# Four edits to the front of a two-block transformer kernel: x laid out by features, query splits moved, eleven convolution taps as ScalarE products, modulation halves side by side

## The reference, cut to what matters

```python
mod_x = silu(c) @ w_ada + b_ada          # and the same for c_ctx: mod_c
hx = rms_norm(x, norm1_g) * (1 + sc1) + sh1
hc = rms_norm(ctx, norm1_g) * (1 + csc1) + csh1
q, k, v, u = split(hx @ w_in)            # kc, vc from hc
attn = softmax([q_rot . k_rot + bias, q . kc]) @ [v, vc]        # 8 heads of 64
conv = silu(layer_norm(depthwise_conv31(u_a * sigmoid(u_b)) + bias))
x = x + g1 * ([attn, conv] @ w_out)
```

## Time and profile before

| | us |
|---|---|
| median of 3 runs | 731.97 (731.96 to 732.14) |
| profiled execution | 731.81 |
| span from its first to its last instruction | 730.0 |
| TensorE busy | 716.6 |
| VectorE busy | 515.8 |
| ScalarE busy | 410.5 |

### The profile page before, as it was taken

The page is one execution under the profiler, slowest core; times in us unless marked ns, Lnnn a source line. Parts: engine busy times, 40 slices in busy tenths (PEclk is TensorE's granted clock), DMA queues, the critical chain, the costliest instruction groups (busy, mean ns, idle before and its releaser), DMA issues.

```text
span 730.0 us, 9710 instructions
## 1 busy us (share of the span) xinstructions
PE 716.6 (98%) x3776; PEld 575.7 (79%) x3776; DVE 515.8 (71%) x908; ACT 410.5 (56%) x693; POOL 24.9 (3%) x44
## 2 busy tenths in 40 slices
PE   7999999999999999999999999999999999999996
PEld 6678884578888888888888777778888888888885
DVE  4678999888666767756898799765857455545544
ACT  4278657986654654546545676675555344344432
POOL 1030012001000000000010000000000000000000
PEclk9999999999999999999999999999999999999999
DMA  9994939616556686744548433443376556555511
GB/s 366 414 367 142 386 109 353 216 58 237 186 186 227 231 279 198 271 152 138 161 151 300 155 116 117 148 179 135 116 231 228 175 179 203 194 174 172 173 57 58
DMA packets 72717, 144.90 MB, mean 198 GB/s; under 512 B 4112, under 2 KB 27664, under 8 KB 71648
## 3 DMA queue, kind: packets, MB, share of 16 engines
q1 hardware_dynamic: 70864, 138.98, 54.1%
q0 software_dynamic: 1520, 5.03, 2.0%
q10 hardware_dynamic: 288, 0.27, 0.1%
HBM read 143.22 MB, written 1.05 MB: 198 GB/s over the span
## 4 chain that ended last, share of the span: by engine, by line
PE 84%; DVE 6%; DMA 4%; ACT 3%; issue 2%; SPq 1%; POOL 0%; POOLq 0%; DVEq 0%
PE bank L433 22%; PE bank L435 21%; PE bank L434 21%; PE bank L754 5%; PE bank L415 4%; PE bank L752 3%; DMA WX<-in_w_ada 2%; DVE cacc L1554 2%; DMA XC<-in_ctx 1%; PE bank L452 1%; PE bank L886 1%; PE bank L908 1%; PE bank L617 1%; DVE WL L1539 1%; PE bank L751 1%
## 5 line engine op out<-in xcount | busy, mean ns | idle before, releaser
L1539 DVE TENSOR_TENSOR WL<-W,WH 128x1024 fp32r<-128x1024 f32 (+2 forms) x222 | 249.5, 1169 | 36.8 <-ACT WH L1039 36.5
L1039 ACT ACTIVATE WH<-W 128x1024 fp32r<-128x1024 f32 (+2 forms) x222 | 211.5, 1011 | 50.2 <-DMA W<-in_w_mlp 36.0
L433 PE MATMUL bank<-WH,AHL 128*128 128x512 f32 (+1 forms) x480 | 189.1, 394 | 0.3 <-DVE AHL L1548 0.3
L435 PE MATMUL bank<-WH,AHL 128*128 128x512 f32 (+1 forms) x480 | 185.4, 386 | 0.0
L434 PE MATMUL bank<-WL,AHL 128*128 128x512 f32 (+1 forms) x480 | 185.2, 386 | 0.0
L433 PEld LDWEIGHTS bank<-WH,AHL 128*128 128x128 f32 x480 | 90.2, 188 | 21.6 <-issue 3.2
L435 PEld LDWEIGHTS bank<-WH,AHL 128*128 128x128 f32 x480 | 90.1, 188 | 18.7
L434 PEld LDWEIGHTS bank<-WL,AHL 128*128 128x128 f32 x480 | 90.3, 188 | 16.9
L433 PE MATMUL bank<-WH,HH 128*128 128x512 f32 (+1 forms) x218 | 84.9, 390 | 0.0
L435 PE MATMUL bank<-WH,HL 128*128 128x512 f32 (+1 forms) x218 | 84.5, 388 | 0.0
L434 PE MATMUL bank<-WL,HH 128*128 128x512 f32 (+1 forms) x218 | 84.4, 387 | 0.0
(11 more groups left out here) (276 smaller groups left out, 853.8 us busy)
## 6 DMA issues: line engine op xcount, KB each, us to landing
W<-in_w_mlp SPq DMA_DIRECT2D x32, 1024.0 KB, 5.5
W<-in_w_in SPq DMA_DIRECT2D x24, 1024.0 KB, 5.7
W<-in_w_gate SPq DMA_DIRECT2D x22, 512.0 KB, 3.9
W<-in_w_up SPq DMA_DIRECT2D x22, 512.0 KB, 5.0
W<-in_w_down SPq DMA_DIRECT2D x11, 1024.0 KB, 4.9
W<-in_w_ada SPq DMA_DIRECT2D x10, 1024.0 KB, 9.1
WX<-in_w_ada SPq DMA_DIRECT2D x10, 1024.0 KB, 11.1
W<-in_w_out SPq DMA_DIRECT2D x8, 1024.0 KB, 5.7
```

The source lines that it names most:

```text
L433: e.matmul(po, hs, wh[:, k, c0:c0 + cw], start=first and k == 0, stop=False)
L435: ins = e.matmul(po, ls, wh[:, k, c0:c0 + cw], start=False, stop=last and k == unit.nk - 1)
L1039: e.activation(m.WH[unit.slot][:, c], m.W32[unit.slot][:, c], ACT.Copy).then_inc(S["w_hi"], 1)
L1539: e.tensor_tensor(m.WL[unit.slot][:, c], m.W32[unit.slot][:, c], m.WH[unit.slot][:, c].bitcast(F32), ALU.subtract).then_inc(S["w_lo"], 1)
```

## The change

x is laid out by features on the host and loaded so; its squares are summed over feature blocks on VectorE and over partitions by one-column matmuls, the factor is spread over partitions by two matmuls with the identity and kept as a tile, and each block is modulated from it; the shift is applied in the split. The sixteen transposes and the two scaled copies of x go. x by rows, still wanted for the residual, is loaded before unit 22. ScalarE splits the query units between the context quarters, and VectorE likewise. Eleven taps in place of eight are products; their additions come at other places among the taps. In the attention loop the two halves of a modulation step stand together behind the probability product, in the last turn the single half stands before it, and one turn of rows uses bank 0. The renaming of one semaphore is left out here.

```diff
@@ -68,6 +68,11 @@
         self.XC = M("XC", 48, [128, 2, D])
+        self.XT = M("XT", 0, [128, 8, 256])
+        self.xsq = M("xsq", 24, [128, 8, 256])
+        self.xpair = [M(f"xpair{i}", 68 + 2 * i, [128, 2, 256]) for i in range(2)]
+        self.xfour = [M(f"xfour{i}", 73 + i, [128, 256]) for i in range(2)]
+        self.rB = M("rB", 72, [128, 256])
         self.XC2 = M("XC2", 56, [128, 2, D])
@@ -186,7 +191,7 @@
-CONV_PRODUCTS = 8
+CONV_PRODUCTS = 11
 OUT_ORDER = [(2, 0), (3, 0), (0, 0), (1, 0), (2, 1), (3, 1), (0, 1), (1, 1)]
@@ -310,12 +315,14 @@
-    for tb in range(2):
-        e.dma_start(m.X[:, tb, :], d["x"][128 * tb:128 * tb + 128, :]).then_inc(S[f"l_x{tb}"], 16)
+    for h in range(2):
+        e.dma_start(m.XT[:, 4 * h:4 * h + 4, :], d["xt"][:, 4 * h:4 * h + 4, :]).then_inc(S[f"l_x{h}"], 16)
     for n in range(14):
...
     for n in range(14, len(units)):
+        if n == 22:
+            e.dma_start(m.X[:, :, :], d["x"].rearrange("(t p) n -> p t n", p=128)).then_inc(S["l_x"], 16)
         load(n)
@@ -351,8 +358,9 @@
     e.memset(m.ones[:, :], 1.0).then_inc(S["fills"], 1)
-    power(0)
-    power(1)
+    w.wait_ge(S["setup"], 2)
+    w.wait_ge(S["mean_sq"], 2)
+    e.tensor_tensor(m.stat[:, 40:42], m.stat[:, 24:26], m.stat[:, 94:95].to_broadcast([128, 2]), ALU.pow).then_inc(S["rstd"], 2)
     power(2)
@@ -479,14 +487,11 @@
         w.wait_ge(S["l_id"], 16)
-        w.wait_ge(S["x_hat"], 2)
-        for tb in range(2):
-            e.transpose(bank[b][:, 256 + tb * 128:384 + tb * 128], m.S1[:, tb, 128 * e8:128 * e8 + 128], m.ident[:, :])
         w.wait_ge(S["rows1_dve"], e8 + 1)
...
         ins.then_inc(S["rows1_turned"], 1)
-        frees(b, ("mx_dve", e8 + 1))
+        frees(b, ("mod1_sum", e8 + 1))
@@ -515,8 +520,31 @@
+    def x_sums():
+
+        for h in range(2):
+            w.wait_ge(S["x_adds"], 2 * h + 2)
+            for tb in range(2):
+                ins = e.matmul(bank[6 + tb][:, 0:1], m.xfour[h][:, tb * 128:tb * 128 + 128], m.ones[:, 0:1], start=h == 0,
+                               stop=h == 1)
+        ins.then_inc(S["sums"], 1)
+
+    def x_spread():
+
+        b = turn_bank("x_spread", 7)
+        w.wait_ge(S["l_id"], 16)
+        w.wait_ge(S["rstd"], 2)
+        for tb in range(2):
+            ins = e.matmul(bank[b][:, tb * 128:tb * 128 + 128], m.stat[:, 40 + tb:41 + tb].to_broadcast([128, 128]),
+                           m.ident[:, :], start=True, stop=True)
+        ins.then_inc(S["sums"], 1)
+        frees(b, ("setup", 5))
+
     keep_busy(16)
+    x_sums()
     mod_first(0)
+    keep_busy(3)
+    x_spread()
     mod_turn(0)
@@ -626,8 +654,8 @@
-    def mod_second_tail(i):
-        b = turn_bank("rows2_turned")
+    def mod_second_tail(i, b=None):
+        b = turn_bank("rows2_turned", b)
         w.wait_ge(S["rows2"], i + 1)
@@ -675,15 +703,19 @@
             scores1(u + 1)
+        if u in (1, 2, 3, 4, 6):
+            mod_second_tail(min(u - 1, 4), 0 if u == 6 else None)
+        if u == 5:
+            conv_mean()
+        if u == 7:
+            mod_second(11)
+        if u:
+            pv1(u - 1)
         if u < 4:
             mod_second(2 * u)
-        if u in (1, 2, 3, 4, 6):
-            mod_second_tail(min(u - 1, 4))
-        if u == 5:
-            conv_mean()
-        if u:
-            pv1(u - 1)
-        mod_second(2 * u + 1 if u < 4 else u + 4)
+            mod_second(2 * u + 1)
+        elif u < 7:
+            mod_second(u + 4)
         if u == 7:
@@ -1057,7 +1089,7 @@
         w.wait_ge(S["mx_dve"], k + 1)
-        copy(m.AH[:, k, :], m.hT[:, k, :], "mx_act")
+        e.activation(m.AH[:, k, :], m.hT[:, k, :], ACT.Identity, bias=m.mod1[:, k, 0, 0:1]).then_inc(S["mx_act"], 1)
@@ -1073,12 +1105,15 @@
+    def half_of(t, h):
+        return t[:, 4 * h:4 * h + 4, :].rearrange("p a b -> p (a b)")
+
     e.dma_start(m.cs[:, :], d["cs"]).then_inc(S["l_cs"], 16)
...
         w.wait_ge(S[f"l_x{tb}"], 16)
-        square(tb, m.X[:, tb, :], m.S1[:, tb, :])
+        e.activation(half_of(m.xsq, tb), half_of(m.XT, tb), ACT.Square, scale=1.0 / 32).then_inc(S["sq_sum"], 1)
     for k in range(6):
@@ -1094,9 +1129,11 @@
         e.activation(m.G[:, tb, :], bank[2 + tb][:, :], ACT.Sigmoid).then_inc(S["gate_sig"], 1)
-    for i in range(1, 4):
-        modulate_c(i, 3 * (i - 1))
-    hi(2)
+    hi()
+    modulate_c(1, 0)
+    hi()
+    modulate_c(2, 3)
+    modulate_c(3, 6)
     for j in range(2):
@@ -1130,7 +1167,7 @@
         from_bank("q_mm", 2 + 2 * tb, m.Q[:, tb, :], 2 + tb, slice(0, 512), "q_out", 0.125)
-    tap_products(4, 5)
+        tap_products(*((5, 6) if tb else (4,)))
     def qk_features(i, dst):
@@ -1138,8 +1175,7 @@
         from_bank("v_mm", 2 * tb + 2, m.VC[:, tb, :], 4 + tb, slice(0, 512), "vc_out")
-        if tb == 0:
-            tap_products(6, 7)
+        tap_products(*((10,) if tb else (7, 8, 9)))
     qk_features(0, m.kcT)
@@ -1593,14 +1629,15 @@
         w.wait_ge(S["mod1"], 2 * k + 2)
-        e.tensor_scalar(m.hT[:, k, :], bank[m.turn_bank["rows1_turned", k + 1]][:, 256:512], m.A1[:, 0, k:k + 1],
-                        m.mod1[:, k, 0, 0:1], ALU.mult, ALU.add).then_inc(S["mx_dve"], 1)
+        w.wait_ge(S["setup"], 5)
+        w.wait_ge(S[f"l_x{k // 4}"], 16)
+        fused(m.hT[:, k, :], m.XT[:, k, :], m.A1[:, 0, k:k + 1], m.rB[:, :], ALU.mult, ALU.mult, "mx_dve")
...
         w.wait_ge(S["mx_act"], k + 1)
-        tt(m.AL[:, k, :], m.hT[:, k, :], m.AH[:, k, :].bitcast(F32), ALU.subtract, "kx")
+        fused(m.AL[:, k, :], m.hT[:, k, :], m.mod1[:, k, 0, 0:1], m.AH[:, k, :].bitcast(F32), ALU.add, ALU.subtract, "kx")
@@ -1622,11 +1659,20 @@
     e.tensor_copy(m.csp[:, :, 0:2], m.cs[:, :].rearrange("p (k r) -> p k r", r=2)).then_inc(S["setup"], 1)
+    for h in range(2):
+        w.wait_ge(S["sq_sum"], h + 1)
+        tt(flat(m.xpair[h][:, :, :]), two(m.xsq, 2 * h), two(m.xsq, 2 * h + 1), ALU.add, "x_adds")
+        w.wait_ge(S["x_adds"], 2 * h + 1)
+        tt(m.xfour[h][:, :], m.xpair[h][:, 0, :], m.xpair[h][:, 1, :], ALU.add, "x_adds")
+    w.wait_ge(S["sums"], 1)
     for tb in range(2):
-        mean_square(tb, (tb,))
-        hat(m.X, m.S1, tb, tb, "x_hat")
+        e.tensor_scalar(col(24 + tb), bank[6 + tb][:, 0:1], EPS, None, ALU.add).then_inc(S["mean_sq"], 1)
+    rows_out(0)
+    w.wait_ge(S["sums"], 2)
+    e.tensor_copy(m.rB[:, :], bank[7][:, 0:256]).then_inc(S["setup"], 1)
     for k in range(8):
-        rows_out(k)
+        if k:
+            rows_out(k)
         modulation(k)
@@ -1645,8 +1691,9 @@
     for i in range(1, 4):
+        if i < 3:
+            lo()
         low_quarter(i, m.hTc, m.CH, m.CL, "c", ("mc_act", 3 * i))
-    lo(2)
@@ -1714,21 +1761,23 @@
     w.wait_ge(S["kc"], 4)
     w.wait_ge(S["k_out"], 2)
     rope1(m.KR, m.Kt, "rotated")
-    taps(8)
+    taps(4)
     add_product()
+    add_product()
+    taps(4)
     add_product()
     taps(8)
     lo(2)
     add_product()
-    taps(4)
+    taps(2)
     add_product()
     w.wait_ge(S["q_out"], 2)
     w.wait_ge(S["rotated"], 1)
     rope1(m.QR, m.Q, "rotated")
-    for n in range(4):
-        taps(6 if n else 2)
+    for n in range(6):
+        taps(4 if n else 0)
         add_product()
-    taps(16)
+    taps(8)
     def soft1(n):
@@ -1825,7 +1874,7 @@
             mod_second_tail(min(u - 1, 4))
-        taps((8, 7, 7, 6, 0, 0, 0, 0)[u])
+        taps((6, 6, 6, 5, 3, 0, 0, 0)[u])
         if u:
@@ -1868,6 +1917,7 @@
         hn = slice(512 * n, 512 * n + 512)
+        w.wait_ge(S["l_x"], 16)
         w.wait_ge(S["out_mm"], OUT_AT[n, tb])
@@ -2337,6 +2387,9 @@
+    def blocks(v):
+        return v.T.reshape(8, 128, 256).transpose(1, 0, 2)
+
@@ -2366,7 +2419,7 @@
-        "vec": vec, "cs": cs, "x": a["x"][0], "ctx": a["ctx"][0], "ident": np.eye(128, dtype=np.float32),
+        "vec": vec, "cs": cs, "x": a["x"][0], "ctx": a["ctx"][0], "xt": blocks(a["x"][0]), "ident": np.eye(128, dtype=np.float32),
...
```

More of the change, by code:

```diff
@@ L146 @@
 sq_sum mean_sq rstd ada1_mm rows1_dve rows1_turned mod1_sum mod1
-x_hat mx_dve mx_act kx c_hat c_turned mc_dve mc_act kc
+x_adds l_x mx_dve mx_act kx c_hat c_turned mc_dve mc_act kc
 a_mm b_mm gate_sig u u_turned hp conv_first conv k_mm q_mm v_mm k_out kc_out q_out v_out vc_out rope_mul rotated qk_turned qk_act
@@ L150 @@
 bias_zero scores1 max1 exp1 rl1 p1_norm p1_norm_act p1_turned pt1 pv1
-conv_prod conv_add conv_pair conv_block conv_sums conv_dve conv_act conv_rs k_conv a2
+conv_prod conv_add conv_pair conv_block sums conv_dve conv_act conv_rs k_conv a2
 out_mm o1_hi o1_lo res1 nscale_dve nscale_act n_turned n_dve n_act kn
@@ L649, in conv_mean @@
         take(5)
-        e.matmul(bank[5][:, 256:512], m.ones[:, :], m.csum[0][:, :], start=True, stop=True).then_inc(S["conv_sums"], 1)
+        e.matmul(bank[5][:, 256:512], m.ones[:, :], m.csum[0][:, :], start=True, stop=True).then_inc(S["sums"], 1)
         conv_reads.append(("conv_dve", 4))
@@ L658, in conv_var @@
```

(8 more changed lines are left out.)

## The result

The changed kernel takes 733.78 us (median of 10 runs, 733.46 to 735.49), the kernel before 732.00 beside it (10 runs): a ratio of 1.0029, with an interval of 1.0021 to 1.0038. It is slower by 1.8 us, above the forecast of 731.9 and above its range. The profiled execution is at 733.76, its span 732.0, 1.95 and 2.0 over those of before. Six of the ten runs lie at 733.46 to 733.80 with a mean granted clock of 0.998 or 0.999, and four at 735.15 to 735.49 with 0.995 or 0.996; what sets these apart shows in the profile of the first experiment.

What follows compares the result with a forecast made beforehand. It took TensorE, busy 716.6 of 730.0 us, as the bound, so only its gaps could shrink. +0.1 + 1.4 - 0.5 - 1.1 = -0.1 us on the profiled 731.81, 0.16 under the runs' median, gave 731.9; range 730.3 to 733.4.

Steps and rivals of the forecast that it cites:

- The start: First loop, x by features: context transfer unmoved, only two operations on its last stretch change; +0.1 us, ends 0 and 1.1.
- the prediction's own sign: First loop: the prediction is wrong if this loop ends anywhere but near 47.9.
- the last stretch: First loop, from context landing to last step's products: ScalarE's cast with a per-partition shift costs +0.08 us; VectorE's changes cancel.
- The longer round trip: Before step 0 of the first loop: first turn up to 1.1 us later, hidden by a weight wait and shorter steps.
- the rival with the unhidden start: First loop: the later first turn is not hidden, +1.0 us more, 732.9; chance 6%.
- The head start: Rotation of k on VectorE: query splits between context quarters let it start at 62.25 instead of 63.98, 1.7 us earlier.
- The hold: First attention scores: eleven products delay the last addition to 104.7, so TensorE waits for ScalarE's copies, +1.4 us.
- the first rival: First scores: additions follow closer, v's copy is not late, so no hold; faster, 730.5 us, chance 19%.
- The row wait: Early attention loop: TensorE's 0.48 us wait for the row copy goes, as VectorE is ready earlier and TensorE later; -0.5.
- Its bound without cover: Same early turn: the half between scores and probability product is missing, and up to its 1.0 us is waited for.
- Late in the loop: End of attention loop: a product gains 0.1 us and a modulation half of 1.0 fills the remaining wait; -1.1.
- The slower rival, no head start at the rotation of k: VectorE starts that rotation at about 63.98 as before, the hold is 3.1 us; 733.6, chance 13%.

Runs made afterwards that it cites:

- e1: The changed kernel with x by features stored in the order in which its two halves are read: 733.77 us, ratio 1.0020.
- e7: The changed kernel with eight products and the order of taps and additions of before: 731.73 us, ratio 0.9994.
- e12: The kernel before with the query splits between the context quarters alone: 731.30 us, ratio 0.9994.
- e4: The kernel before with the halves of the second modulation together alone: 732.55 us, ratio 1.0005.
- e9: The changed kernel with ScalarE's table load moved behind both copies that VectorE waits for: 733.01 us, ratio 1.0020.
- the two-by-two: The kernel before with query splits, halves apart or together, table load ahead or behind: apart 731.30 and 732.05 us, together 730.98 and 729.74.
- e6: The changed kernel with only the attention output's copy moved ahead of ScalarE's table load: 734.25 us, ratio 1.0036.
- e2: The changed kernel with x by rows as before, the rest of the change kept: 732.79 us, ratio 1.0006.

## Why the prediction was wrong, step by step

**The start, +0.1, measured +1.15.** The failed sentence is that the bytes ahead of the context transfer are the same, both in rows of 4 KB. They are, but lie 8 KB apart, and that slows the first transfers (e1). By the prediction's own sign it was wrong there: the first loop ended at 48.94, not near 47.9. The rest of that step held. Of what was priced on the last stretch, +0.08, 0.15 came (8.52 for 8.37). The longer round trip is hidden: with x contiguous the product of step 1 starts at 12.53, before at 12.37. So the rival with the unhidden start came true in its size, but by a transfer, not by the round trip that it priced. The Trainium skill (DMA: Bandwidth & Descriptors, section Latency and other measured facts) gives rates of copies between HBM tensors that fall as the row pitch grows from 512 KiB to 4 MiB, and advises padding the pitch or laying tiles out contiguously. The trace agrees with the advice at a pitch of 8 KB, by the 123 and 197 GB/s above.

**The head start, 1.7.** Right: the rotation at 62.35 in the frame of before, against 62.3.

**The hold, +1.4, measured 1.85.** The chain of taps, additions and copies was right: 1.49 without the gap of VectorE before the last addition. That gap was in no row. The clock behind the hold was missed altogether: in e1's profile it adds 1.56 us, and four runs of the changed kernel lie about as far, 1.7, above the others. The Trainium skill's cycles (VectorE: DVE Perf Modes, section on the TRN2 errata) gave an estimate of about 0.9; the spacing of the rows was nearer. The Trainium skill's rule (ScalarE: Activation LUTs, section Rules for kernel authors) that additions and multiplications stay on VectorE would have pointed the right way (e7 is 2.05 us faster), though its time, that of the first rival, 730.5, did not come, and it was the additions on VectorE and the shared buffer that cost, not ScalarE's products.

**The row wait, -0.5, measured -1.04 up to the fifth turn.** Right in its cause, VectorE's earlier first softmax (107.77 for 109.38 in e12); too small, since turns with the halves side by side take 5.55 us instead of 5.69. Its bound without cover, up to 1.0, was right too (0.96 in e4).

**Late in the loop, -1.1.** Right where it was looked for: the out projection is 1.0 earlier against the product before it. The failed sentence is in the first part: behind 151 the stretches are full, so the question is by how much the out projection moves. A full stretch only says that its inputs came in time for the old start. They hung on a chain of ScalarE and VectorE that the change does not bring forward: it came 1.95 later, like the turns before it, so 1.10 went back by 171.84 (e9, and the two-by-two).

Of the three sizes, +1.05, +0.45 and +1.1, less 0.54, comes the difference of 2.06 between forecast and measured shift at the last landmark. The slower rival, no head start at the rotation of k, did not happen, though its time of 733.6 is close.

## What to carry to other kernels

A stage in which the engine is full is not a stage with slack: before a gain ahead of it is counted, look when its last inputs arrive and which engines make them. Two edits can be worth little or less than nothing apart and more together: on the stretch 0.38 and -0.58 alone, 1.42 together. So a two-by-two tells more than undoing one part. A new layout should be stored in the order in which it is read, above all for the first transfers: here the context rows, queued far behind them, inherited 1.08 us of delay.

## What the runs showed of the hardware

TensorE's clock can fall behind a single wait: after 1.87 us of standing e1's profile has it at 0.50 for some 3 us, where before the wait it was full. Of 35 runs of the kernels with a hold of 1.8 us (changed, e1, e6, e9), 12 have a mean clock of 0.996 or less; of 11 runs with a hold of 1.49 (e2), none; of the 214 others with a clock on record, seven. This is a count, and a profile of one case; it shows no threshold, and why the same wait leaves the clock whole in the other runs stays open.
